# Searching expert keys in quarters of two heads, with three quarters of pass 0 inside its gather loop

## The reference

```python
def chunk(xc):                                   # 128 tokens
    q = (xc @ wq).reshape(c, PEER_HEADS, 2, PEER_QDIM // 2)
    sc = jnp.einsum('thpd,hpkd->thpk', q, keys)
    top_v, top_i = lax.top_k(sc, PEER_TOPK)
    cand = (top_v[:, :, 0, :, None] + top_v[:, :, 1, None, :]).reshape(c, PEER_HEADS, -1)
    cand_id = (top_i[:, :, 0, :, None] * N_KEYS + top_i[:, :, 1, None, :]).reshape(c, PEER_HEADS, -1)
    best_v, best_pos = lax.top_k(cand, PEER_TOPK)
    ids = jnp.take_along_axis(cand_id, best_pos, axis=-1)
    gate = jax.nn.softmax(best_v, axis=-1)
    act = jax.nn.gelu(jnp.einsum('td,thkd->thk', xc, u_tab[ids])) * gate
    return jnp.einsum('thk,thkd->td', act, v_tab[ids])
```

## Time and profile before

| what | value |
|---|---|
| runs of the kernel before | 1836.35 us median of 3 (1835.11 to 1844.07) |
| profiled execution | 1842.02 us, of which the span of instructions is 1839.1 |
| busy share of the span | PE 81%, DVE 63%, POOL 59%, ACT 21% |
| mean granted TensorE clock | 0.905 |

### The profile page before, as it was taken

One profiled execution on the slowest core, in us unless ns is written; L12 is line 12 of the kernel. 1 busy time (PEld: TensorE's weight loads), 2 busy tenths in 40 slices (PEclk: granted clock), 3 DMA queues, 4 the chain that ended last, 5 costly groups with the idle time before them and its releaser, 6 DMA issues.

```text
span 1839.1 us, 15963 instructions
## 1 busy us (share of the span) xinstructions
PE 1493.1 (81%) x4780; PEld 799.9 (43%) x4780; DVE 1157.0 (63%) x2646; ACT 389.9 (21%) x991; POOL 1082.8 (59%) x1028
## 2 busy tenths in 40 slices
PE   6758379889898589889998579879998778777777
PEld 3546235445474234445464234445455433232332
DVE  6644954867469943877468933876648965445453
ACT  2221012233221121233221111233221121111111
POOL 0000345767666655777666655666766667777774
PEclk9768789989998889988999889999998988999889
DMA  7415589989999999999999999999999989999997
GB/s 307 160 35 207 204 359 380 399 297 363 373 401 408 340 418 409 405 369 385 374 401 408 336 415 351 395 340 331 374 376 405 369 301 410 409 409 409 407 388 307
DMA packets 179053, 649.87 MB, mean 353 GB/s; under 512 B 17783, under 2 KB 19319, under 8 KB 174105
## 3 DMA queue, kind: packets, MB, share of 16 engines
q0 software_dynamic: 147456, 536.94, 76.0%
q1 hardware_dynamic: 31512, 111.92, 15.7%
HBM read 644.07 MB, written 4.72 MB: 353 GB/s over the span
## 4 chain that ended last, share of the span: by engine, by line
PE 41%; DVE 32%; DMA 13%; issue 8%; POOL 4%; ACT 2%; DVEq 0%; SPq 0%; POOLq 0%
PE ps L1112 21%; DVE junk L865 12%; DMA ring_u<-table_u,ids 11%; PE ps L934 8%; PE ps L1069 3%; POOL ring_v L1143 2%; PE ps L1082 2%; DMA ring_v<-table_v,ids 1%; PE ps L999 1%; POOL ring_u L1138 1%; DVE W L690 1%; DVE W L842 1%; DVE W L844 1%; DVE W L845 1%; PE ps L1009 1%
## 5 line engine op out<-in xcount | busy, mean ns | idle before, releaser
L1112 PE MATMUL ps<-ring_v,diag 128*128 128x512 f32 x2048 | 982.4, 636 | 229.2 <-ACT diag L480 227.6
L865 DVE CUSTOM_DVE_ANT_0 junk<-ring_u,h 128x1024 bf16<-128x1024 f32 x512 | 627.4, 1225 | 268.1 <-DMA ring_u<-table_u,ids 212.5
L1138 POOL DMA_INDIRECT ring_u<-table_u,ids x512 | 536.1, 1047 | 387.7 <-DVE ids L849 204.9
L1143 POOL DMA_INDIRECT ring_v<-table_v,ids x512 | 546.5, 1067 | 352.2 <-PE ps L1112 269.9
L1112 PEld LDWEIGHTS ps<-ring_v,diag 128*128 128x128 f32 x2048 | 412.0, 205 | 761.4 <-issue 751.6
L471 ACT ACTIVATE acts<-dots 128x4 f32<-128x4 f32 x128 | 26.3, 205 | 998.6 <-DVE dots L865 998.6
L480 ACT ACTIVATE diag<-cst,weights 128x128 f32<-128x128 f32 x512 | 163.5, 390 | 39.2 <-DVE weights L874 39.0
L934 PE MATMUL ps<-W,hT 128*128 128x384 f32 (+2 forms) x384 | 142.9, 531 | 4.0 <-DVE hT L576 2.6
L1082 PE MATMUL ps<-hT,W 128*128 128x128 f32 x1024 | 117.7, 276 | 2.7 <-DVE hT L576 2.6
L1082 PEld LDWEIGHTS ps<-hT,W 128*128 128x128 f32 x1024 | 116.0, 192 | 3.8 <-DVE hT L576 3.8
L934 PEld LDWEIGHTS ps<-W,hT 128*128 128x128 f32 x384 | 73.7, 193 | 72.3 <-issue 36.9
(11 more groups left out here) (247 smaller groups left out, 1050.4 us busy)
## 6 DMA issues: line engine op xcount, KB each, us to landing
W<-w_in SPq DMA_DIRECT2D x32, 1282.0 KB, 15.2
W<-peer_wq SPq DMA_DIRECT2D x16, 2048.0 KB, 21.0
W<-w_out SPq DMA_DIRECT2D x4, 4096.0 KB, 19.5
ring_u<-table_u,ids POOLq DMA_INDIRECT x512, 7.8
ring_v<-table_v,ids POOLq DMA_INDIRECT x512, 7.7
W<-keys_t SPq DMA_DIRECT2D x4, 1024.0 KB, 8.3
zkv<-gain_mix SPq DMA_DIRECT2D x4, 512.0 KB, 16.0
toep<-ring_u SPq DMA_DIRECT2D x1, 2048.0 KB, 7.4
```

What stands on the lines that cost most here:

```text
L865: v.tensor_tensor_reduce(junk[:, :], ring_u[:, s, :], h[:, b, :], 1.0, 0.0, ALU.mult, ALU.add, dots[:, s:s + 1]).then_inc(dots_done, 1)
L1112: mm = pe.matmul(ps[:, c, :], diag[:, s, :], ring_v[:, s, c * 512:(c + 1) * 512], start=False, stop=False, skip_group_check=True)
L1138: gp.indirect_dma_start(ring_u[:, k % RING, :], None, table_u, bass.IndirectOffsetOnAxis(ap=ids[:, b, k:k + 1], axis=0)).then_inc(u_in[k % ...
L1143: gp.indirect_dma_start(ring_v[:, k % RING, :], None, table_v, bass.IndirectOffsetOnAxis(ap=ids[:, b, k:k + 1], axis=0)).then_inc(v_in[k % ...
```

## The change

Pairs and ids now work on quarters of two heads (QH = 2, QS = 32 experts), q = 0 to 3, each as soon as its own score is there. The buffers, the semaphore counts and the waits follow: POOL waits for ids_ready at i = 0, 8, 16 and 24, and SP for four quarters a pass. The list of the mix keeps 30 entries, of which the last eight are now score and quarter in turn. The other part is the order: of the mix of pass 0 only the entries up to the first quarter stand ahead of its loop. The six left (three scores with queries 2 and 3, three quarters) go into that loop, and the mix of pass 1 behind them. Where more entries are left than groups, a group takes two (turns): i = 0, 1 and 2 take a score and a quarter each, i = 3 takes the norm and the first projection step of pass 1, and from i = 4 on each group takes one, the last at i = 31. The loops of passes 1 and 2 keep one entry a group, the last at i = 29.

```diff
-    search = [["out 0"], ["out 1"], ["norm 1", "rows 1"], ["query 0"], ["score 0", "query 1"], ["score 1", "query 2"],
-              ["pairs 0"], ["ids 0"], ["score 2", "query 3"], ["score 3"], ["pairs 1"], ["ids 1"]]
+    search = [["out 0"], ["out 1"], ["norm 1", "rows 1"], ["query 0"], ["score 0", "query 1"], ["pairs 0", "ids 0"],
+              ["score 1", "query 2"], ["pairs 1", "ids 1"], ["score 2", "query 3"], ["pairs 2", "ids 2"],
+              ["score 3"], ["pairs 3", "ids 3"]]
...
+    first = mix.index(["pairs 0", "ids 0"]) + 1
     do(mix[:1] + [["phases 0", "tables 0", "phases 1"]] + mix[1:k] + [["turned 0"]] + mix[k:k + 1] + [["lines"]]
-       + mix[k + 1:out] + [["tables 1"]] + mix[out:out + 2] + [["turned 1"]] + mix[out + 2:], 0)
+       + mix[k + 1:out] + [["tables 1"]] + mix[out:out + 2] + [["turned 1"]] + mix[out + 2:first], 0)
     for n in range(PASSES):
-        left = list(mix) if n + 1 < PASSES else []
+        left = [(group, n) for group in mix[first:]] if n == 0 else []
+        if n + 1 < PASSES:
+            left += [(group, n + 1) for group in mix]
...
+            turns = -(-len(left) // (HALVES - i))
...
-            do(left[:1], n + 1)
-            left = left[1:]
+            for group, of in left[:turns]:
+                do([group], of)
+            left = left[turns:]
...
                 if n:
-                    sp.wait_ge(ids_ready, 2 * n)
+                    sp.wait_ge(ids_ready, QUARTERS * n)
...
-                four = [(4 * q + i, cand[:, i, :]) for i in range(4)]
-                for k, c in four:
+                two = [(QH * q + i, cand[:, i, :]) for i in range(QH)]
+                for k, c in two:
...
-                    step(v.tensor_tensor(hit.rearrange("p n k a -> p (n k) a"), bc(posf[:, half], 2, TOPK),
-                                         bc(cst[:, C_IOTA:C_IOTA + TOPK], 1, SLOTS // 2), ALU.is_equal))
+                    step(v.tensor_tensor(hit.rearrange("p n k a -> p (n k) a"), bc(posf[:, part], 2, TOPK),
+                                         bc(cst[:, C_IOTA:C_IOTA + TOPK], 1, QS), ALU.is_equal))
...
-                    if i % (HALVES // 2) == 0:
-                        gp.wait_ge(ids_ready, 2 * n + i // (HALVES // 2) + 1)
+                    if i % (HALVES // QUARTERS) == 0:
+                        gp.wait_ge(ids_ready, QUARTERS * n + i // (HALVES // QUARTERS) + 1)
```

More of the change, by code:

```diff
@@ L39 @@
 HALVES = SLOTS // RING_G
+QUARTERS = 4
+QH = PH // QUARTERS
+QS = SLOTS // QUARTERS
 IN_SPLIT = [GW, GW, GW, NH, GW, GW, GW, GW, GW, GW, GW]
@@ L151, in plan_steps @@
             plan.append(("weigh", n, i))
-            late = not (left and left[0][0].startswith("norm"))
+            turns = -(-len(left) // (HALVES - i))
+            late = not (left and left[0][0][0].startswith("norm"))
             if not late:
                 plan.append(("rows of v", n, i))
-            do(left[:1], n + 1)
-            left = left[1:]
+            for group, of in left[:turns]:
+                do([group], of)
+            left = left[turns:]
             if late:
@@ L461, in find_ids @@
             def find_ids(n, q):
-                half = gates[:, n % NB, q * SLOTS // 2:(q + 1) * SLOTS // 2]
-                a.wait_ge(best_sub, 2 * n + q + 1)
-                a.activation(half, half, ACT.Exp).then_inc(gate_exp, 1)
+                part = gates[:, n % NB, q * QS:(q + 1) * QS]
+                a.wait_ge(best_sub, QUARTERS * n + q + 1)
+                a.activation(part, part, ACT.Exp).then_inc(gate_exp, 1)
             def take_dots(n, i):
@@ L827, in find_ids @@
             def find_ids(n, q):
-                b, heads, half = n % NB, slice(4 * q, 4 * q + 4), slice(q * SLOTS // 2, (q + 1) * SLOTS // 2)
-                g3 = by(gates[:, b, half], TOPK)
+                b, heads, part = n % NB, slice(QH * q, QH * q + QH), slice(q * QS, (q + 1) * QS)
+                g3 = by(gates[:, b, part], TOPK)
+                total = small[:, 400:400 + QH]
                 v.tensor_tensor(g3, best[:, heads, :], bc(best[:, heads, 0], 2, TOPK), ALU.subtract).then_inc(best_sub, 1)
-                step(v.tensor_copy(i16f[:, 8 * q:8 * q + 8, :], i16[:, 8 * q:8 * q + 8, :]))
@@ L834, in find_ids @@
-                pos_f = pos.rearrange("p n k -> p (n k)")[:, half]
-                i4 = i16f[:, 8 * q:8 * q + 8, :].rearrange("p (n s) k -> p n s k", s=2)
+                step(v.tensor_copy(i16f[:, 2 * QH * q:2 * QH * (q + 1), :], i16[:, 2 * QH * q:2 * QH * (q + 1), :]))
+                pos_f = pos.rearrange("p n k -> p (n k)")[:, part]
+                i4 = i16f[:, 2 * QH * q:2 * QH * (q + 1), :].rearrange("p (n s) k -> p n s k", s=2)
                 for s in range(2):
                     if s == 0:
-                        step(v.tensor_single_scalar(posd[:, half], pos_f, 4, op=ALU.logical_shift_right))
+                        step(v.tensor_single_scalar(posd[:, part], pos_f, 4, op=ALU.logical_shift_right))
@@ L839, in find_ids @@
                     else:
-                        step(v.tensor_single_scalar(posd[:, half], pos_f, TOPK - 1, op=ALU.bitwise_and))
-                    step(v.tensor_copy(posf[:, half], posd[:, half]))
-                    step(v.tensor_tensor(hit.rearrange("p n k a -> p (n k) a"), bc(posf[:, half], 2, TOPK),
-                                         bc(cst[:, C_IOTA:C_IOTA + TOPK], 1, SLOTS // 2), ALU.is_equal))
+                        step(v.tensor_single_scalar(posd[:, part], pos_f, TOPK - 1, op=ALU.bitwise_and))
@@ L844, in find_ids @@
+                    step(v.tensor_copy(posf[:, part], posd[:, part]))
+                    step(v.tensor_tensor(hit.rearrange("p n k a -> p (n k) a"), bc(posf[:, part], 2, TOPK),
+                                         bc(cst[:, C_IOTA:C_IOTA + TOPK], 1, QS), ALU.is_equal))
                     step(v.tensor_tensor(hit, hit, bc(i4[:, :, s, :], 2, TOPK), ALU.mult))
-                    step(v.reduce_sum(idf[s][:, half], hit.rearrange("p n k a -> p (n k) a"), AX))
-                step(v.scalar_tensor_tensor(out=idf[0][:, half], in0=idf[0][:, half], scalar=float(NK), in1=idf[1][:, half],
+                    step(v.reduce_sum(idf[s][:, part], hit.rearrange("p n k a -> p (n k) a"), AX))
@@ L847, in find_ids @@
+                step(v.scalar_tensor_tensor(out=idf[0][:, part], in0=idf[0][:, part], scalar=float(NK), in1=idf[1][:, part],
                                             op0=ALU.mult, op1=ALU.add))
[L848 to L851, removed]
@@ L852, in find_ids @@
-                step(v.reciprocal(small[:, 400:404], small[:, 400:404]))
-                v.tensor_tensor(g3, g3, bc(small[:, 400:404], 2, TOPK), ALU.mult).then_inc(gates_ready, 1)
-                v.wait_ge(gates_ready, 2 * n + q + 1)
+                step(v.tensor_scalar(idf[0][:, part], idf[0][:, part], row[:, R_LC + 2:R_LC + 3], None, ALU.add))
+                v.tensor_copy(ids[:, b, part], idf[0][:, part]).then_inc(ids_ready, 1)
+                v.wait_ge(gate_exp, QUARTERS * n + q + 1)
+                step(v.reduce_sum(total, g3, AX))
@@ L856, in take_dots @@
+                step(v.reciprocal(total, total))
+                v.tensor_tensor(g3, g3, bc(total, 2, TOPK), ALU.mult).then_inc(gates_ready, 1)
+                v.wait_ge(gates_ready, QUARTERS * n + q + 1)
             def take_dots(n, i):
```

14 lines of the change are left out of this document (7 added, 7 removed).

## The result

The changed kernel takes 1849.53 us, the median of 20 runs, against 1838.9 us of the kernel before, the median of 20 runs beside them. The ratio is 1.0057, with a 95% interval of 1.0041 to 1.0072. It is slower, by some 10 us, where I had forecast no change.

A forecast was written before the change was run, and what follows sets the result against it. No engine was taken to bound the loop throughout: PE at its head, DVE in the search, DMA behind it. Pass 0's -3.6 us and +1.6 for each of two searches gave -0.4: 1836 us beside the 1836.35 median, range 1821 to 1849.

The forecast's parts named there:

- The head of pass 0: Ahead of pass 0's loop: ids of quarter 0 at 186.9 us, first dots end at 199.3, norm's dots at 261.6.
- the wide operations of the ids: In each quarter's ids: six operations, 0.68 us each on 512 elements instead of 1.23 on 1024, saving 3.3 us.
- the second score that finds PE ready: In searches inside a loop: with a quarter between the scores, DVE's 3.7 to 3.8 us wait on PE goes.
- DMA alone: Rival, chance 0.22 with partial forms: DMA alone paces the loop, only the 17.5 us earlier gather counts, 1819 us.
- The third rival: Seam of pass 0, chance 0.06: the projection waits for the last w_in chunk and loses 10.6 us, 1847 us.
- Part 1: Search on DVE: a quarter takes 11.5 us, so four take 46.0 against 39.4 for two halves, 6.6 more a search.
- Part 4: Search inside a loop: the vanished wait on PE leaves 1.6 us of the 6.6 on the path.
- the sum: Whole kernel: pass 0 -3.6 us, searches of passes 2 and 3 +1.6 each, together -0.4 us.
- Part 3: Rest of pass 0's loop: mix 19.2 us late from the first projection's end, the following 25 groups unchanged until the search.
- Part 5: Seam to pass 1: projection 19.9 us behind the search instead of 44.4, at 677.1 us, 3.6 earlier, no w_in wait.
- the growth by more than 3 us in a pass: Sign of being wrong: a shift of the seams that grows by more than 3 us a pass.
- quarters paid in full: Rival, chance 0.10: score 1 still waits on PE, all 6.6 us show in three searches, 1851 us.

The follow-up runs named there:

- quarters_pass0: Changed kernel with quarters in pass 0 alone, interleaved in its loop, and halves in passes 1 to 3: 1844.19 us, ratio 1.0013 to the kernel before.
- gaps_in_attention: Kernel before, with the two groups without mix in the loops of passes 0 and 1 moved from behind the search into the attention: 1821.37 us, ratio 0.9917.
- again: The changed kernel, unaltered, measured once more against the kernel before: 1846.59 us against 1842.32, ratio 1.0033.
- halves_in_loop: Changed kernel with halves in all passes; the second half of pass 0's search stands in its loop: 1836.57 us, ratio 0.9959 to the kernel before.
- quarters_ahead: Changed kernel with quarters in all passes, but the whole search of pass 0 ahead of its loop: 1856.68 us, ratio 1.0098 to the kernel before.
- search3_quarters: Kernel before with quarters only in the search of pass 3, in the loop of pass 2: ratio 1.0040.
- search2_quarters: Kernel before with quarters only in the search of pass 2, in the loop of pass 1: ratio 1.0021.

## Why the prediction was wrong

The window of the three in-loop quarters in after, with the columns as above:

```profile
190.00:261.00 71.00, 37.14 (x128) 20.79 (x128) 64.56 (x232) 13.79 (x26) 37.52 (x37) 0.76 0.79 285
```

What stood. The head of pass 0 in every row but the length of a quarter, the wide operations of the ids, the second score that finds PE ready, a seam 25 us shorter, and no wait for w_in although its cover shrank. Of the rivals, DMA alone is refuted: in the window of the three in-loop quarters DMA moves 285 GB/s, below the 376 of the earlier trace rows, and quarters_pass0 shows that the earlier first gather does not even pay for the quarters that allow it. The third rival's wait is not in the chain: the chunks landed 8.7 to 29.4 us after their issue, a little sooner than in the earlier trace rows. The rule of the Trainium skill that I had set against this ("DMA: Bandwidth & Descriptors", Queues, rings and completion order) agrees with the trace in its turns, though the wait that I drew from it did not come. Six chunks were issued from 660.45 to 662.82 us in after, and four gathers of table_u from 662.09 to 667.07. The gathers landed so:

```profile
DMA to landing us min/median/max: 10.4/14.1/19.7
```

The last of them landed at 667.07 + 19.7 = 686.8, ahead of the last chunk, which was issued some 4 us before it and landed at 662.82 + 29.4 = 692.2. So gathers do take their share from the chunks, and the 24.96 us of one gather did not speak against turns, as I had read them; yet the first chunk was there after 8.7 us, and nothing waited for it.

What failed. The step that failed most is the price of a quarter (Part 1) and what was built on it, 1.6 us left of each search (Part 4 and the sum): a quarter takes 11.9 to 12.3 us and not 11.5, and a search leaves 3.9 to 4.3 us. The second is the 25 groups of Part 3 that I held unchanged, which took 2.4 us more. I forecast -3.6 us at the projection behind pass 0 and found 679.48 + 2.96 - 680.72 = +1.7. The steps, each against its forecast:

- **The quarter (Part 1), 11.9 to 12.3 us instead of 11.5.** The pairs take 5.1 instead of 4.9 and the ids 6.7 to 7.2 instead of 6.6, since the many small operations on 32 elements last as long as those on 64 (0.18 to 0.24 us), and some inside the loop 0.35. The Trainium skill has this ("VectorE: DVE Perf Modes", The TRN2 errata: a fixed cost that every instruction pays, whatever its size), and the trace agrees: 0.19 us on 32 elements, 0.69 on 512. My line priced the wide operations rightly; the small ones I had let off with 0.3 us as if nearly free. Three quarters inside the loop, and a head 0.9 us late, put the dots ahead of the norm at 261.00 + 2.96 = 263.96 instead of 261.6: +2.4. When w_out is issued, +1.7 of it is left.
- **The 25 groups that I called unchanged (Part 3), +2.4.** From the w_out load to that of the query weights before takes 189.35 us, after 191.75:

```profile
326.63:518.38 191.75, 168.61 (x539) 92.78 (x539) 128.13 (x231) 55.74 (x137) 129.12 (x120) 0.93 0.95 355
```

  The counts and DVE's 128.1 us are those of before (its row stands with gaps_in_attention); PE is busy 168.61 us instead of 166.47 for the same 539 matmuls, at a mean granted clock of 0.93 instead of 0.94. The same stretch takes 191.8 to 192.0 us in again, halves_in_loop, quarters_pass0 and quarters_ahead, 189.5 in search3_quarters, but 191.0 in search2_quarters, which is the kernel before up to there. So it follows no single part of the change. The five long ones all differ from before in the search of pass 0; whether that or chance moves the clock is open. PE's busy time carries 2.1 of the 2.4 us; in search2_quarters it does not (166.47 us busy, as before), so chance alone can bring 1.6 us.
- **The search in the loop (Part 4), +3.9 for pass 1 instead of +1.6.** In that of pass 2 four quarters are 11.90 + 12.22 + 11.90 + 12.34 = 48.4 us where I had 46.0, and DVE waits 0.9 us for rows. Against before: 9.0 us more of search, less 3.7 of PE's wait and 1.0 of DMA's, +4.3. The hidden part was right; the price of a quarter, 0.6 us too low, was off four times a search.
- **The seam (Part 5), 18.9 us instead of 19.9**, 1.0 less.

Together 1.7 + 2.4 + 2.3 - 1.0 = 5.4, against the 5.3 that are missing.

For the later passes I had charged 1.6 for each search. That of pass 2 costs +4.3 at its end but only +1.0 from projection to projection, because the wait for DMA at its seam shrinks from 25.02 to 19.93 us. That of pass 3 costs +4.2 and keeps it, the growth by more than 3 us in a pass that I had named as a sign of being wrong. So 1.7 + 1.0 + 4.2 = 6.9 us at the start of the last loop in after, and 7.2 in again by the same rows, against -0.4 forecast. The timed ratios say 10.5 and 6.1 us. The rest of the 10.6 us between the two profiled spans is 4.8 in the last loop, which the change doesn't touch, less the 2.96 of the start, with some 2 us from the last group on. One stretch of that loop in after:

```profile
1650.00:1700.00 50.00, 34.31 (x70) 14.05 (x69) 22.54 (x41) 7.41 (x25) 39.02 (x37) 0.91 0.99 372
```

In after DMA falls to 372 GB/s in this stretch; in before a like stretch stands at 1770 to 1800 us, in quarters_ahead there is none there. From group 0 to group 31 the last loop takes 330.4, 332.3 and 331.3 us in after, again and quarters_pass0, and 323.4 to 329.1 in the seven other profiles of these chips. The three are those with quarters in the loop of pass 0, more than 1200 us earlier; I know of no way in which that could reach so far, and three profiles are too few. Whether the change lengthens the last loop is left open; the timed ratios, 1.0057 and 1.0033, leave room for it.

The rival "quarters paid in full", 1851 us, came nearest to the time, but by another way: its condition, a second score that still waits for PE, did not come about. And what decided the size of the whole is a thing that I had split wrongly: the gain did not come from the early start but from taking groups 30 and 31 out of the seam. gaps_in_attention shows it without any early start, and halves in the same order as the change gain 5 to 8 us; quarters in pass 0 cost at least 3.7 of it, and those of pass 3 another 4.

## What to carry to other kernels

Cutting a serial stage of one engine into smaller pieces costs its small operations once more for each piece (here 9 to 10 us a search); read for each place whether a wait for something else stands right behind it, since only there is the extra work free. Where bulk loads share the queue, don't leave iterations without other work beside them: the same two bare groups cost 25.2 to 26.9 us beside the w_in loads and 12.7 to 19.3 in the attention, but 27.0 and 24.7 on a chip where DMA had no room left. And ask of an earlier start what paces the stretch behind it; if that isn't what was started earlier, as here, the start repays little.

## What the hardware showed that I had not expected

- The rate of the same gather differs by chip: 409 GB/s in undisturbed stretches of one, 350 to 366 in the same loop of another, with the whole kernel at 1914.74 us instead of 1838.9. A gain of 0.83% on one was 0.50% on the other, though with intervals that overlap.
- Even on the faster chips, stretches of 30 to 100 us in the last loop run at 349 to 390 GB/s in most profiles, at differing places; quarters_ahead and gaps_in_attention have none.
- A gather issued behind six w_in chunks does not wait for all of them: it landed 19.7 us after its issue, ahead of the last chunk, which took 29.4.
- The same 539 matmuls take 166.5 us on TensorE in one profile and 168.6 in another, at mean granted clocks of 0.94 and 0.93. In a third profile the stretch is 191.0 us long instead of 189.4, with PE busy for 166.5 us.
